# A head's attention output is copied raw from PSUM first; half and remainder are made from that copy, and its output product comes one step later

## The reference, cut to what matters

```
layer 0: proj = h @ w_in
         NSA, 8 heads: o = g0*softmax(q.k_cmp)v_cmp + g1*softmax(q.k_slc)v_slc + g2*softmax(q.k_win)v_win
         MLA, 8 heads: o = softmax((q_nope.k_nope + q_pe.k_pe)*scale) v
         mix = concat(o_nsa, o_mla) @ ev_w_out              (16 heads x 128 = 2048 rows)
layer 1: DSA, 16 heads: o = softmax(q.k*scale + bias, masked to the top 64 keys) v
         mix = concat(o) @ od_w_out
both:    x = x + gate * mix, then x = x + gate * conv_ffn(...)
```

## Time and profile before

| what | value |
|---|---|
| median of 3 runs | 2067.17 us (2065.99 to 2078.59) |
| profiled execution | 2075.76 us, its span 2073.6 us, mean granted TensorE clock 0.968 |
| PE busy | 1903.3 us (92%) |
| PEld busy | 1636.3 us (79%) |
| DVE busy | 1556.4 us (75%) |
| ACT busy | 1045.0 us (50%) |
| POOL busy | 204.5 us (10%) |
| chain that ended last | PE 74%, DVE 12%, DMA 9%, ACT 3%, issue 1% |

### The profile page before, as it was taken

One profiled execution on the slowest core, in us unless ns is written; L12 is line 12 of the kernel. 1 busy time (PEld: TensorE's weight loads), 2 busy tenths in 40 slices (PEclk: granted clock), 3 DMA queues, 4 the chain that ended last, 5 costly groups with the idle time before them and its releaser, 6 DMA issues.

```text
span 2073.6 us, 34020 instructions
## 1 busy us (share of the span) xinstructions
PE 1903.3 (92%) x11444; PEld 1636.3 (79%) x11444; DVE 1556.4 (75%) x2447; ACT 1045.0 (50%) x2225; POOL 204.5 (10%) x317
## 2 busy tenths in 40 slices
PE   3179998889999999999999989989999999999998
PEld 2058853667699999997777777768799999998787
DVE  4987743677778888889787878878777777778554
ACT  1144445554555555556444546555555555556443
POOL 1220000442100000000011000033000000000000
PEclk9679999899999999999999999999999999999999
DMA  8979984566488888876899686868667777765555
GB/s 329 398 267 316 336 298 142 203 207 245 159 287 281 266 285 268 280 264 231 299 340 321 221 298 195 277 229 293 226 226 230 223 225 241 225 204 176 177 189 176
DMA packets 210967, 521.25 MB, mean 251 GB/s; under 512 B 23041, under 2 KB 43010, under 8 KB 186018
## 3 DMA queue, kind: packets, MB, share of 16 engines
q1 hardware_dynamic: 180722, 316.19, 46.8%
q0 software_dynamic: 28032, 201.44, 26.7%
q10 hardware_dynamic: 2096, 2.12, 0.3%
HBM read 517.53 MB, written 2.12 MB: 251 GB/s over the span
## 4 chain that ended last, share of the span: by engine, by line
PE 74%; DVE 12%; DMA 9%; ACT 3%; issue 1%; SPq 0%; DVEq 0%; POOLq 0%; ACTq 0%
PE ps L1024 12%; PE ps L1020 12%; PE ps L1021 11%; PE ps L923 10%; PE ps L919 10%; PE ps L920 9%; DVE acc L1685 5%; DVE ring_lo L1763 2%; DMA ring<-in_od_w_in 2%; DMA first_ring<-in_ada_w 2%; DMA ring<-in_ev_w_in 2%; PE ps L758 1%; PE ps L1116 1%; DMA aring<-in_ada_w 1%; DMA ring<-in_ffn_w_down 1%
## 5 line engine op out<-in xcount | busy, mean ns | idle before, releaser
L1233 ACT ACTIVATE ring_hi<-ring 128x512 fp32r<-128x512 f32 (+2 forms) x1152 | 689.5, 621 | 601.9 <-DMA ring<-in_ffn_w_up 231.1
L1763 DVE TENSOR_TENSOR ring_lo<-ring,ring_hi 128x512 fp32r<-128x512 f32 (+2 forms) x1152 | 742.4, 682 | 292.6 <-ACT ring_hi L1233 291.5
L1020 PE MATMUL ps<-hT_hi,ring_hi 128*128 128x256 f32 x2048 | 512.8, 283 | 1.5 <-issue 0.4
L1021 PE MATMUL ps<-hT_lo,ring_hi 128*128 128x256 f32 x2048 | 507.9, 280 | 0.0
L1021 PEld LDWEIGHTS ps<-hT_lo,ring_hi 128*128 128x128 f32 x2048 | 387.8, 189 | 0.0
L1020 PEld LDWEIGHTS ps<-hT_hi,ring_hi 128*128 128x128 f32 x2048 | 385.4, 188 | 2.4 <-issue 1.2
L1024 PE MATMUL ps<-hT_hi,ring_lo 128*128 128x256 f32 x2048 | 330.0, 282 | 2.4 <-DVE ring_lo L1763 2.4
L1024 PEld LDWEIGHTS ps<-hT_hi,ring_lo 128*128 128x128 f32 x2048 | 280.0, 188 | 2.6 <-DVE ring_lo L1763 2.6
L1685 DVE SCALAR_TENSOR_TENSOR acc<-aring,cs,acc 128x2048 f32<-128x2048 f32 x112 | 263.4, 2352 | 19.9 <-DMA aring<-in_ada_w 8.3
L920 PE MATMUL ps<-ring_hi,hT_lo 128*128 128x512 f32 (+2 forms) x640 | 244.9, 384 | 0.0
L642 POOL DMA_DIRECT2D aring<-in_ada_w x176 | 94.3, 536 | 1402.1 <-DVE acc L1685 1376.6
(11 more groups left out here) (240 smaller groups left out, 1975.8 us busy)
## 6 DMA issues: line engine op xcount, KB each, us to landing
aring<-in_ada_w POOLq DMA_DIRECT2D x176, 1024.0 KB, 6.8
ring<-in_ffn_w_up SPq DMA_DIRECT2D x512, 256.0 KB, 2.9
ring<-in_ffn_w_down SPq DMA_DIRECT2D x256, 256.0 KB, 3.2
ring<-in_od_w_in SPq DMA_DIRECT2D x112, 256.0 KB, 3.7
ring<-in_ev_w_in SPq DMA_DIRECT2D x80, 256.0 KB, 5.5
first_ring<-in_ada_w POOLq DMA_DIRECT2D x16, 1024.0 KB, 7.2
ring<-in_ev_w_out SPq DMA_DIRECT2D x64, 256.0 KB, 3.3
ring<-in_od_w_out SPq DMA_DIRECT2D x64, 256.0 KB, 4.2
```

The costliest lines, as they stand in the source:

```text
L1020: nc.tensor.matmul(o[q], hi, hT_hi[:, kt, :], start=start, stop=False, skip_group_check=True)
L1021: nc.tensor.matmul(o[q], hi, hT_lo[:, kt, :], start=False, stop=False, skip_group_check=True)
L1233: ins = nc.scalar.activation(out_, in_, f, **kw)
L1763: put(v.tensor_tensor(ring_lo[:, g, part], ring[:, g, part], ring_hi[:, g, part].bitcast(F32), ALU.subtract), lo_ok)
```

## The change

When a head's output is complete, ScalarE first copies the bank raw into `hT[:, kt]` (raising `o_out`), then rounds from that copy into `head_both` (raising `o_hi`); the second instruction waits for the first (`chain=True`). VectorE subtracts the half from the raw copy, in place, and raises a new semaphore `o_lo`. TensorE's `values` still waits for `o_out`, which now is the raw copy; the output product waits for `o_lo`. `SPLIT_AT` goes from 4 to 5 and `PRODUCT_AT` from 6 to 7, so the two `high`, the two `low` and the output product of each head come one step later, and TensorE's loop has one more step (its length is `len(units) + PRODUCT_AT`).

```diff
--- before.py
+++ after.py
@@ -469,7 +469,8 @@
                 self.w_ok = sig(f"{tag}_w_ok")
                 self.scaled = sig(f"{tag}_scaled")
                 self.t_ok, self.pt_ok = sig(f"{tag}_t_ok"), sig(f"{tag}_pt_ok")
-                self.o_ok, self.o_hi, self.o_out = sig(f"{tag}_o_ok"), sig(f"{tag}_o_hi"), sig(f"{tag}_o_out")
+                self.o_ok, self.o_out = sig(f"{tag}_o_ok"), sig(f"{tag}_o_out")
+                self.o_hi, self.o_lo = sig(f"{tag}_o_hi"), sig(f"{tag}_o_lo")
                 self.last_of = [n for n in range(len(units)) if n + 1 == len(units) or self.qh[n + 1] != self.qh[n]]
                 self.first_of = [0] + [n + 1 for n in self.last_of[:-1]]
                 self.kt = [h + (NSA_H if kind == "mla" else 0) for kind, h in (units[n] for n in self.first_of)]
@@ -506,7 +507,7 @@
                 return side_r[:, ST * KVF:ST * (KVF + QF)].rearrange("p (t n) -> p t n", t=ST)[:, :, at:at + HD]
             return wide_r[:, 0:ST * E_COLS].rearrange("p (t n) -> p t n", t=ST)[:, :, E_Q + h * HD:E_Q + (h + 1) * HD]
 
-        SPLIT_AT, PRODUCT_AT = 4, 6
+        SPLIT_AT, PRODUCT_AT = 5, 7
 
         def products_at(att, n):
 
@@ -811,7 +812,7 @@
                     output(n - LAG)
                 rotary(n + 1)
                 for q, b in products_at(att, n):
-                    pe.wait_ge(att.o_out.handle, q + 1)
+                    pe.wait_ge(att.o_lo.handle, q + 1)
                     product(q, b)
                 if 0 <= n - LAG - 1 < len(units):
                     values(n - LAG - 1)
@@ -1411,7 +1412,9 @@
                     q = head_at(att, n, LAG + 2)
                     if q is not None:
                         act.wait_ge(att.o_ok.handle, n - LAG - 1)
-                        run(att.o_hi, head_both(att, q), ps[:, O_B, 0:S].rearrange("p (t s) -> p t s", t=ST), ACT.Copy)
+                        raw = hT[:, att.kt[q], :]
+                        run(att.o_out, raw, ps[:, O_B, 0:S], ACT.Copy)
+                        run(att.o_hi, head_both(att, q), raw.rearrange("p (t s) -> p t s", t=ST), ACT.Copy, chain=True)
 
                 queries(0)
                 for n in range(len(units) + LAG + 2):
@@ -1937,8 +1940,8 @@
                     if q is not None:
                         dve.wait_ge(att.o_hi.handle, q + 1)
                         put(v.tensor_tensor(hT_lo[:, att.kt[q], :].rearrange("p (t s) -> p t s", t=ST),
-                                            ps[:, O_B, 0:S].rearrange("p (t s) -> p t s", t=ST),
-                                            head_both(att, q).bitcast(F32), ALU.subtract), att.o_out)
+                                            hT[:, att.kt[q], :].rearrange("p (t s) -> p t s", t=ST),
+                                            head_both(att, q).bitcast(F32), ALU.subtract), att.o_lo)
 
                 for n in range(len(units) + LAG + 3):
                     if 0 <= n - 1 < len(units):
```

## The result

The changed kernel took a median of **2078.15 us** (20 runs, 2068.47 to 2085.54), the kernel before 2069.84 us beside it (20 runs, 2058.06 to 2078.71). The ratio is 1.0038, with an interval of 1.0024 to 1.0052: the change costs about 8 us (5 to 11). That is less than the 1% (about 21 us) that the prediction counts as no change, but it is a cost clear of the noise and not the near nothing (+2.4 us) of the forecast.

The account below looks back on a forecast made before the run. TensorE was busy 92% of the span, and its 17.3 us of waits for the remainder capped the direct gain. Terms 0.9 + 0 + 0.1 + 1.4 = +2.4 us on the 2067.17 us median gave 2069.6 us, range 2061 to 2080.

Parts of the forecast that it names:

- the odd end's bound: End of odd attention: last head's pair stands behind an adaLN product awaiting its DMA; +1.4 us, upper bound +3.
- Short periods: Even-attention periods without an adaLN product in B: 16.42 us, a gain of 0.86 us each.
- Now 6.33 - 4.23 + 1.41 = 3.51: Short periods, slc's logits to win's logits: 6.33 us with three products becomes 3.51 us with one.
- Long periods: Even-attention periods with an adaLN product in B: win's logits wait for VectorE's slc logits; 18.44 us, 1.16 us longer.
- Even tail: End of the even attention, up to the gate sums: 20.96 us before, 20.9 us after, a change of 0.
- Odd attention: Stage with one head a step: +0.1 us at its start, +1.4 us at its end.
- B: The cmp step of an even-attention period (mla, cmp, slc, win); the change moves its one product to the slc step.
- 1, the adaLN product of B stays hidden: Even attention: all six periods gain 0.86 us, 5.2 us, and the odd end costs nothing; 2062 us, chance 0.18.
- 2, the whole wait is gained: Attention stages: TensorE's whole wait for the remainder, 17.3 us, becomes gain; 2050 us, chance 0.03.
- 3, GpSimd and VectorE block each other: Odd attention: remainder waits out GpSimd's first scaling, 0.6 us more a step, +2.7 us in all; 2072.3 us, chance 0.12.
- 4, the clock: Early odd attention: TensorE's low clock reaches the first step with products, +4.9 us; 2074.5 us, chance 0.10.
- 5, no decoupling: Values wait for ScalarE's raw copy as long as for the remainder; +11 us for uncovered copies, 2078 us, chance 0.02.

Follow-up runs that it names:

- e5: Changed kernel with eight idle matmuls of zeros in each step B of the even attention, five ahead of values, three behind; 2071.46 us, ratio 1.0009 to the kernel before.
- e4: Changed kernel without the adaLN product in even-attention steps 8, 16 and 24, done after the attention instead; 2078.37 us, ratio 1.0039 to the kernel before.
- e3: Changed kernel with sixteen idle matmuls of zeros in each step B of the even attention, ten ahead of values, six behind; 2077.46 us, ratio 1.0034 to the kernel before.
- e2: Kernel before with roundings, weight remainders and out-products one step later, without the raw copy; 2082.60 us, ratio 1.0060 to the kernel before.
- e1: Changed kernel with the raw copy, but roundings, weight remainders and out-products back in their old steps; 2064.08 us, ratio 0.9982 to the kernel before.
- e8: Kernel before with seven idle matmuls of zeros ahead of values in step B of the even attention; 2066.21 us, ratio 0.9977 to the kernel before.
- e7: e1 without the adaLN product in even-attention steps 8, 16 and 24, done after the attention instead; 2071.96 us, ratio 1.0009 to the kernel before.
- e6: e1 with seven idle matmuls of zeros behind values in each step B of the even attention; 2062.05 us, ratio 0.9953 to the kernel before.

## Why the prediction was right, and where its sizes were off

The class (no change that counts) and the range of 2061 to 2080 us held; the central value was 6 to 8.5 us low: 8.5 against 2069.6 us itself, 6 if the +2.4 us are put on the median of 2069.84. The likeliest case had been given 2066 to 2073 us, and 2078.15 lies outside it. That it lies inside the wide range is partly luck: the top of that range was made of the odd end's bound, of rivals 3 and 4 and of the slowest run of before, and the excess came from none of these. The order of events was right in both stages, and what the sum lacked was the clock of the even one.

**Short periods: the order of events right, the size wrong.** Forecast 16.42 us, measured 17.93, 17.93 and 17.70: 4.3 us more in all. The step that failed is "Now 6.33 - 4.23 + 1.41 = 3.51". It took full-speed matmuls from the earlier trace rows for a stretch in front of which the change itself had opened a hole; at the low clock the stretch took 5.14 us. At full clock it takes 3.54 us, with the hole filled (e5) and with the hole open (the first period of e4, from 381.36 to 384.90). "Period lengths alternate between 18.4 and 16.4 us" became 18.9 and 17.9.

**Long periods: right, 0.5 us too short.** Win's logits at 9.88 us (9.79) behind VectorE; 18.90, 19.12 and 18.89 us against 18.44, together 1.6 us more. e3 and two of e5's have the same 18.9 us at full clock. The row of L726 with its 0.43 us for ScalarE's q copy is the likely place, and all three long periods of e5 have that wait too; that it comes from the copies or roundings that now stand ahead on ScalarE was not tested.

**Even tail: forecast 0, measured +3.3, most of it clock.** The sum had 11.5 us to the end of the last NSA values; it was 13.2 (483.23 to 496.40), of which the time to the first values was even less than assumed (2.93 us, not 3.3), while L958 at 488.57 shows 1.06 us instead of 0.63. The second part had 4.65 us to the half pair and took 4.77 (to 501.17), with the wait of 2.08 us that it implies; behind it 4.70 us of products took 6.29 (L958 at 503.42: 1.05 us). That is 1.7 and 1.6 us, with the order of events as worked out. Of the first, 1.2 us are clock: in e5, whose fill covers the hole ahead of it, the part is 12.0 us. The other 0.5 us is a size that the sum had wrong. The second is all clock: in e4, where the clock did not fall there, the same products took 4.72 us (503.13 to 507.85).

**Sum for the even attention.** 0.9 forecast + 4.3 + 1.6 + 3.3, and 0.2 in the ramp: 10.3, measured 10.2. Of the 9.3 us that were missing, about 7 are clock (4.3, 1.2 and 1.6).

**Odd attention: the size right, the place wrong.** The forecast of +1.5 reaches to L923 behind the gate sums, where TensorE had been idle for 1.08 us. Up to the gate sums the same working gives +2.6 us (0.1, and products that end at 1454.3 instead of 1451.80); measured there, in the two first profiles, +2.5. Behind the gate sums TensorE no longer waits, as the working had it. The four kernels with copy and shift have 90.5 to 91.6 us up to the gate sums (mean 91.0), the five without the shift 88.1 to 90.0 (mean 89.2): +1.8. e2, with the shift alone, has 89.95. The half pair behind an adaLN product that waits for its DMA is there (2.29 us, then 1.60 us of L958), two heads earlier than I had put it: at 1443.00, not at the last head. Such a wait, of 0.7 to 1.7 us, stands in all four kernels with copy and shift and in none of the other six ahead of the gate sums. That kind of wait was forecast and its place not.

**ScalarE's copies: right.** 0.38 and 0.42 us, the second 0.41 us behind the first:

```profile
444.53 0.38 ACT L1234 ACTIVATE hT<-ps 128x256 f32<-128x256 f32 x1 [2.57 <-PE ps L803]
444.94 0.42 ACT L1234 ACTIVATE wide_r<-hT 128x256 fp32r<-128x256 f32 x1
```

The forecast had 0.35 for the added one. The 8.6 us that L790 waits for the raw copy are not lost: the 0.71 us wait for VectorE's logits of B ends later still, as the working had it, so slc's logits start at 4.33 us (4.26). And in e1, which has the copies and not the shift, the even attention is 3.5 us shorter than before.

**The rivals.** 1, the adaLN product of B stays hidden: no, win's logits wait behind it. 2, the whole wait is gained: no; B's logits held TensorE, as argued. 3, GpSimd and VectorE block each other: it is there, and its cost is not. The remainder suffers beside GpSimd's scaling in the odd attention, by 0.25 us at most where 0.6 were put down, and TensorE is full there:

```profile
1386.66 0.93 POOL L689 TENSOR_SCALAR L<-L,rw 128x256 f32<-128x256 f32 x1
```

```profile
1386.76 0.66 DVE L1942 TENSOR_TENSOR hT_lo<-hT,wide_r 128x256 fp32r<-128x256 f32 x1
```

In the even attention it is GpSimd that suffers, in step B of nearly every period of the kernels with the raw copy, and in none of before, e2 and e8. After, then before:

```profile
433.05 1.56 POOL L689 TENSOR_SCALAR L<-L,rw 128x256 f32<-128x256 f32 x1
```

```profile
420.27 0.93 POOL L688 TENSOR_SCALAR L<-L,rw 128x256 f32<-128x256 f32 x1
```

No period pays for it: the first one of e4 has it too (1.56 us) and lasts the 16.45 us of the forecast. The prediction also read the earlier trace rows as showing that both slow down; they show it for VectorE alone.

The Trainium skill (SBUF — State Buffer, section "Who interferes with whom", on the shared port pair) has the loser blocked wholly. For VectorE the trace does not agree: its remainder began 0.10 us after a scaling and took 0.66 us, so it was slowed and not held until the scaling's end. For GpSimd the 0.63 us more are about one of the two subtracts of the pair, which a whole block would give as well.

**4, the clock: the right mechanism in the wrong stage.** It had +4.9 us at the odd start, where nothing of the kind came; it came in five of the six even periods and twice in the tail, where the earlier trace rows hold the same pattern of a drained TensorE, and where the working had just shown that step B loses its product. Its own price of a half-speed stretch should have been asked of each step that the change empties. 5, no decoupling: its time, 2078 us, is the measured one by coincidence only. L790 does wait as long for the raw copy as L789 for the remainder before (8.6 and 9.0 us), but another wait ends behind it, and the waits of L797 (7.3 us) shrink to 0.5 us (L798).

**What stays open.** Which stop makes the clock fall. The rows ahead of a fall and of none can be the same: in after's first period and in e4's first TensorE has the same two idle stretches in B as in the later ones, and the clock did not fall. In e1 and e7 it fell in every second period, with or without the product in B. The kernel before has holes of its own; there it fell once in the six periods (from 467.86, in one of 17.17 us, which did not pay) and once in the tail. What is shown is that it fell in most periods of the kernels with the open hole and in nearly none of those with the hole filled, and what a fall costs. How often it falls is known by place from one execution of each kernel, and over all executions only as the mean clock of the second table.

## What to carry to other kernels

Before moving an engine's work out of a step, look at what the step is left with: a hole in TensorE's row can cost not only itself but the speed of the matmuls behind it, and in a sum made of full-speed rows it doesn't show. Undo the two halves of a change apart: here the copy alone was better than the whole change, and a handful of idle matmuls in the remaining hole brought more. Among the periods of one profile look for one in which the suspect is missing: it is a control for which nothing has to be built. When single profiles of two kernels agree although their medians don't, compare stage by stage, and leave out the stages that the change doesn't touch.

## What the runs showed of the hardware that was not expected

- TensorE's granted clock can fall to 1.2 GHz once in each of many short loop rounds, between stretches at 2.4 GHz: 27.3 of 134.7 us between step 7 and the gate sums in after, 41.0 of 143.1 in e2, none in e6. No idle stretch of TensorE in those periods of after was longer than 1.85 us.
- A low clock right in front of a wait for another engine costs next to nothing (long periods of after: 18.90 us without it, 18.89 and 19.12 with it); in front of TensorE's own work it cost 1.3 to 1.6 us for 3.4 us of low clock (e4: 16.45 against 17.74 to 18.08 us).
- Eight idle matmuls of 128x128 in a period (1.28 + 0.94 us in the rows of e5) kept 2.4 GHz in five of six; in the sixth it fell behind a hole that they do not cover, and that one took 20.47 us.
- A VectorE subtract with both inputs in SBUF and GpSimd's scaling slow each other, and which of them suffers changes from place to place: 0.66 instead of 0.42 us for the subtract at 1386.76, 1.56 instead of 0.93 us for the scaling at 433.05.
